# Two transformer blocks on one core: reciprocals, modulation parts, output slab quarters and first maxima in another order

## The chip, the cores and the metric

The kernel runs on 1 core of one Trainium2 chip. The metric is the device time of one execution in microseconds (us). The engines are TensorE (PE; its weight loads are PEld), VectorE (DVE), ScalarE (ACT), GpSimd (POOL) and SyncE (SP), which here only issues DMAs.

## What is computed

A first block with adaptive modulation, a token mixer of sparse attention (8 heads of 64, keys chosen by an indexer) beside a short convolution, and a SwiGLU; then a second block of two layers: gated linear attention, and differential attention (8 heads of two score maps each), each followed by a SwiGLU and a gated per-layer term. There are 256 tokens of width 1024, all in float32. The two parts that matter here, cut down:

```python
# first block, per 128-query block: the chosen keys are the causal top 64 of the indexer's scores
logits = einsum('bqhd,bqkd->bhqk', q_b, kg) * attn_scale
p = softmax(where(valid, logits, NEG_INF)); o = einsum('bhqk,bqkd->bqhd', p, vg)
mod = silu(c) @ w_ada + b_ada            # 6144 columns: shifts, scales and gates
mixed = concat([group_rms_norm(attn), group_rms_norm(gate_b * conv)]) @ w_out
# differential attention, per head: two softmaxes, their difference, values
o = (softmax(q1 @ k1.T) - lam * softmax(q2 @ k2.T)) @ v      # then rms_norm per head, then @ w_out
```

## The kernel before

The whole program is written out by hand for each engine. Every engine has one in-order stream, and semaphores join the streams; nothing is reordered by a compiler. All activations lie transposed, 128 channels x 256 tokens a tile, eight tiles a tensor.

**Weight slabs.** A large product takes its weights as slabs of 128 x 4096 values (2 MB). For a product at float32 precision a slab and its operand are split into a high and a low part (`whi`, `wlo`; `ohi`, `olo`), and TensorE runs three matmuls for each pair of tiles (`three`, L2219 to L2221). A slab is split in four quarters of 1024 columns. ScalarE writes the high quarter (`split`, called by `ahead`, L899), VectorE the low one (`low`, L1464); `lo_ready` counts the low quarters, and SyncE loads the next slab into a raw buffer when it is free. `ahead(ph, at, 0)` first waits until the slab that lies in the high buffer has been used by TensorE.

**Modulation parts.** The product `silu(c) @ w_ada` is done by VectorE. Its last eight slabs come in parts of 512 KB, four to a slab, and `modulate_part(n)` (L1561, L1563) adds part n: two operations of 512 columns, each chained to the next. `part_used` counts the parts done. TensorE sums a finished slab over its partitions (`modulation(i)`). On SyncE part 18 and 19 are loaded early; part 20 waits for `part_used` 19 (part 18 done), 21 for 20, 22 for 21, 23 for 22. SyncE's order around them is: parts 18, 19, 20, then `load_out(1)` (the second slab of the first block's output product, `out_w1`, which itself waits for `part_used` 18), then parts 21, 22, 23, then the first slab of `gate_up0`.

**Heads of the first block** (i = 0 to 7). TensorE: scores of head i+1; a projection of 16 matmul records (`in_hc` for i below 4, then `in_gb`); in head 5 the group sums of the first squares; the transposes of head i (`turned`, L2501), which need the scaled probabilities; the values of head i-1; now and then a modulation slab; in head 6 the group sums of `mix_sq` 2 (L2333), which need ScalarE's squares. ScalarE: scale head i's probabilities (L1075, waits for `inverted`), exponentials of head i+1 (L1063, wait for `max_ready`), `beside_head(i)`, the copy of the transposes (`prob_t`). `beside_head` has in heads 5 and 6 a high quarter of `out_w1`, and in head 6 the squares of tiles 4 and 5 ahead of it. VectorE: the loop that the diff changes, with `masked_maxima` (L1704, L1707), `invert_sums` (L1714), the convolution (L1650 to L1653) or the gated product (L1676), the low quarters and the parts. In heads 5 and 6 it has `low(PH["out0"], At(1), i - 5)`, which waits for ScalarE's high quarter.

**Differential heads** (i = 0 to 7, and three rounds to drain). TensorE: scores of head i+1 (L2820), values of head i-2 (L2835), six steps of the value projection (`value_steps`), transposes of head i-1 (L2846). Scores of head i+1 use the banks of head i-1 and wait for its exponentials. ScalarE: exponentials of head i (L1409), the copy of the transposes of head i-1 (L1425), in rounds 2, 5 and 7 `take_values` (L1385), then the high quarter of the output slab. VectorE: maxima of head i (L2166, L2169), the copy of head i-3's output (L2173), the probabilities of head i-1 (L2178 to L2185), then a low quarter. Before the heads stand `turn(6)` and `turn(7)`, the last two rotations of the keys (L2128, L2132), which take a product from GpSimd (L859).

Of the kernel before, what the change touches and what calls it, by code (L numbers as in the profile page):

```python
# [35 lines left out]
HD = 64  # L36
# [236 lines left out]
def build(nc, a, out):  # L273

    ctx = ExitStack()
    with ctx:
# [592 lines left out]
        def _(act):  # L869
# [32 lines left out]
            def ahead(ph, at, q):  # L902

                nxt = follow(ph, at)
                if nxt is None:
                    return
                if q == 0:

                    wait(act, tile_done, at.lin(ph.tile0, ph.tiles))
                split(*nxt, q)  # L910
# [490 lines left out]
            for i in range(NH + 1):  # L1401
                if i < NH:
                    me.next(max_ready)
                    for c in range(2):
                        for qt in range(2):
                            n = 4 * (i % 2) + 2 * c + qt
                            if i >= 2:
                                act.wait_ge(trans_done, NH + i - 1)
                            ins = act.activation(tl(d_p, 4 * (i % 2) + 2 * c + qt),  # L1409
                                                 G[2 * (i % 2) + c][:, qt * T:(qt + 1) * T], ACT.Exp,  # L1410
                                                 bias=neg_max[:, n:n + 1], scale=HD ** -0.5,
                                                 accum_out=sums[:, n:n + 1])
                        me.did(ins, exp_done)
                if i == 5:
                    squares((0,), d_o, d_nsq)
                if i == 7:
                    pair_root(0, X[1])
                    squares((1,), d_o, d_nsq)
                if i >= 1:
                    me.next(trans_done)  # L1420
                    if i == 1:
                        act.wait_ge(qk_ready, 8)
                    if i >= 3:
                        act.wait_ge(pv_done, NH + i - 2)
                    me.did(act.activation(tl(d_pt, (i - 1) % 2, w=512), X[0][:, :], ACT.Copy), pt_ready)  # L1425
                if i in (2, 5, 7):
                    take_values({2: 1, 5: 2, 7: 3}[i])
                if 1 <= i <= 4:
                    ahead(*OUT2, i - 1)
            wait(act, tile_done, PH["diff_v"].tile0 + 4)  # L1430
            high_parts_of(0, 1)
            pair_root(1, X[1])
# [22 lines left out]
        def _(dve):  # L1455
            me = Steps(dve, dve_step)

            def low(ph, at, q):

                slot, w = (ph.slot + at.parity) % 2, ph.cols // 4  # L1460
                hslot = (ph.j0 + at.parity) % 2
                src = out_w[hslot] if ph.name == "out0" else raw[slot]
                dve.wait_ge(hi_ready, at.lin(4 * ph.j0 + q + 1, 4))
                dve.tensor_tensor(wlo[hslot][:, q * w:(q + 1) * w], src[:, q * w:(q + 1) * w],  # L1464
                                  whi[hslot][:, q * w:(q + 1) * w].bitcast(F32), ALU.subtract).then_inc(lo_ready, 1)
# [245 lines left out]
            def invert_sums(i):  # L1711
                me.next(exp_done)
                s = i % 2
                me.did(dve.reciprocal(rsum[:, 2 * s:2 * s + 2], sums[:, 2 * s:2 * s + 2]), inverted)  # L1714

            PARTS_OF_HEAD = ((11, 12), (13, 14), (15, 16), (17, 18), (19, 20), (21,), (22,), (23,))
            me.again()
            masked_maxima(0)
            for q in range(2):
                low(PH["out0"], At(0), q)  # L1720
            modulate_part(10)
            for i in range(NH):
                invert_sums(i)
                if i + 1 < NH:
                    masked_maxima(i + 1)
                if i == 6:
                    mix_norm(0, 1)
                if i == 7:
                    mix_low(0, 1)
                if i in (1, 2):  # L1730
                    low(PH["out0"], At(0), i + 1)
                if i < 4:
                    short_conv(i)
                else:
                    gated_conv(i - 4)
                    if i in (5, 6):
                        low(PH["out0"], At(1), i - 5)
                for n in PARTS_OF_HEAD[i]:
                    modulate_part(n)
            dve.wait_ge(mod_done, 9)  # L1740
# [404 lines left out]
            VALUES, OUT2 = (PH["diff_v"], At(1)), (PH["out2"], At(0))  # L2145
            low(*VALUES, 0)
            low(*VALUES, 1)
            turn(6)
            turn(7)
            make_tile = group_make(d_o, d_nsq, lambda t: lam[:, 5:6])  # L2150

# [7 lines left out]
                    me.did(low_part(t, tl(om, t), xhi, xlo), olo_ready)  # L2159

            for i in range(NH + 3):
                if i < NH:
                    me.next(score_done)
                    s = 4 * (i % 2)
                    for c in range(2):
                        me.did(dve.tensor_reduce(neg_max[:, s + 2 * c:s + 2 * c + 2],  # L2166
                                                 v3(G[2 * (i % 2) + c][:, :], 2), AX, ALU.max, negate=True))
                    me.again()
                    me.did(dve.tensor_scalar(neg_max[:, s:s + 4], neg_max[:, s:s + 4], HD ** -0.5, None, ALU.mult),  # L2169
                           max_ready)  # L2170
                if i >= 3:
                    me.next(pv_done)
                    me.did(dve.tensor_copy(tl(d_o, i - 3), X[2][:, 0:T]), mixed_ready)  # L2173
                if 1 <= i <= NH:

                    me.next(exp_done, 2)
                    s = 4 * ((i - 1) % 2)
                    me.link(dve.reciprocal(rsum[:, s:s + 4], sums[:, s:s + 4]))  # L2178
                    me.did(dve.tensor_scalar(rsum[:, s + 2:s + 4], rsum[:, s + 2:s + 4], lam[:, 4:5], None, ALU.mult))
                    for qt in range(2):  # L2180
                        me.did(dve.tensor_scalar(tl(d_p, s + qt), tl(d_p, s + qt), rsum[:, s + qt:s + qt + 1],
                                                 None, ALU.mult))
                    me.again()
                    for qt in range(2):
                        ins = dve.scalar_tensor_tensor(tl(d_p, s + qt), tl(d_p, s + 2 + qt),  # L2185
                                                       rsum[:, s + 2 + qt:s + 3 + qt], tl(d_p, s + qt),
                                                       ALU.mult, ALU.add)
                    me.did(ins, prob_ready)
                if i == NH:
                    wait(dve, tile_done, PH["diff_v"].tile0 + 4)  # L2190
                    make_pair(0)
                if i == NH + 1:
                    low_pair(0)
                if i in (0, 1):
                    low(*VALUES, 2 + i)
                if 2 <= i <= 5:
                    low(*OUT2, i - 2)
            for g in range(1, 4):
                make_pair(g)
                if g > 1:  # L2200
# [699 lines left out]
```

## Time and profile before

| what | value |
|---|---|
| median of 3 runs | 1079.1 us (1078.55 to 1080.32) |
| the profiled execution | 1077.96 us, its span 1076.2 us |
| TensorE busy | 1042.4 us, 97% of the span |
| VectorE, ScalarE, GpSimd busy | 731.7, 552.9, 202.2 us |
| mean granted TensorE clock | 0.995 |
| chain that ended last | PE 56%, DVE 5%, ACT 3%, issue 1% |

The page gives shares over the whole span. For an order change the useful views are the engines' waits in a stretch, and the timeline of one engine in that stretch. In a timeline the bracket behind an instruction is the time that its engine stood idle before it, and what released it.

### The profile page before, as it was taken

The page shows a single profiled execution, that of the slowest core. Times are in us where ns is not written, and L with a number is a line of the kernel's source. Part 1 is how long each engine was busy: PE and PEld are TensorE (multiplying, and loading weights), DVE is VectorE, ACT ScalarE, POOL GpSimd, SP SyncE. Part 2 cuts the span into 40 slices and gives each one's busy share as a digit, 9 for nine tenths or more (in the row PEclk, how much of TensorE's full clock was granted, in tenths as well). Part 3 has the DMA queues.
Part 4 walks back from the last instruction along what each step waited for, and adds up shares of the span by engine and source line. Part 5 has one row for each costly group of instructions (what it writes and reads, how often), then busy time and mean ns, then how long its engine had stood idle before and what let it go on. Part 6 is the DMA issues. An engine that isn't in the chain of part 4 may idle for free.

```text
span 1076.2 us, 20430 instructions
## 1 busy us (share of the span) xinstructions
PE 1042.4 (97%) x7993; PEld 981.9 (91%) x7993; DVE 731.7 (68%) x1155; ACT 552.9 (51%) x946; POOL 202.2 (19%) x223
## 2 busy tenths in 40 slices
PE   5999999999999999999999999999989999999998
PEld 5577788999999998989999999998877999999998
DVE  5798777767654788868556555686787765564565
ACT  2223457545363585527454444566467764544453
POOL 0000012233311001022333321021210223322010
PEclk9999999999999999999999999999999999999999
DMA  9993453577556454504564546654322265644661
GB/s 350 399 389 121 169 184 98 195 254 262 174 168 190 137 192 173 183 2 153 186 209 156 174 131 203 247 185 157 131 105 79 93 222 178 212 132 140 185 208 40
DMA packets 183587, 192.78 MB, mean 179 GB/s; under 512 B 5913, under 2 KB 143426, under 8 KB 183522
## 3 DMA queue, kind: packets, MB, share of 16 engines
q1 hardware_dynamic: 182512, 191.15, 52.5%
q8 instruction: 43, 0.70, 0.3%
q0 software_dynamic: 144, 0.52, 0.2%
q10 hardware_dynamic: 866, 0.21, 0.1%
q14 instruction: 22, 0.18, 0.0%
HBM read 190.83 MB, written 1.05 MB: 178 GB/s over the span
## 4 chain that ended last, share of the span: by engine, by line
PE 56%; DVE 5%; ACT 3%; issue 1%; POOL 0%; DVEq 0%; POOLq 0%; ACTq 0%
PE gemm L2219 17%; PE gemm L2221 17%; PE gemm L2220 16%; DVE wlo L1464 1%; PE aux L2717 1%; PE aux L2835 1%; PE aux L2767 1%; ACT whi L899 1%; DVE prod L1943 1%; PE gemm L2820 1%; PE aux L2773 0%; PE aux L2219 0%; DVE state L2075 0%; PE aux L2221 0%; PE aux L2220 0%
## 5 line engine op out<-in xcount | busy, mean ns | idle before, releaser
L2219 PE MATMUL gemm<-ohi,whi 128*128 128x256 f32 x1376 | 389.5, 283 | 3.8 <-issue 1.1
L1464 DVE TENSOR_TENSOR wlo<-raw,whi 128x1024 fp32r<-128x1024 f32 (+1 forms) x308 | 352.2, 1187 | 58.8 <-ACT whi L899 58.1
L2220 PE MATMUL gemm<-olo,whi 128*128 128x256 f32 x1376 | 385.8, 280 | 0.0
L2221 PE MATMUL gemm<-ohi,wlo 128*128 128x256 f32 x1376 | 383.6, 279 | 0.0
L899 ACT ACTIVATE whi<-raw 128x1024 fp32r<-128x1024 f32 (+1 forms) x308 | 276.4, 963 | 60.4 <-PE gemm L2221 44.2
L2219 PEld LDWEIGHTS gemm<-ohi,whi 128*128 128x128 f32 x1376 | 259.1, 188 | 6.7 <-DVE wlo L1464 2.8
L2220 PEld LDWEIGHTS gemm<-olo,whi 128*128 128x128 f32 x1376 | 259.5, 189 | 0.6 <-issue 0.5
L2221 PEld LDWEIGHTS gemm<-ohi,wlo 128*128 128x128 f32 x1376 | 259.4, 189 | 0.0
L2221 PE MATMUL gemm<-acthi,wlo 128*128 128x256 f32 x528 | 147.8, 280 | 0.0
L2219 PE MATMUL gemm<-acthi,whi 128*128 128x256 f32 x528 | 147.5, 279 | 0.0
L2220 PE MATMUL gemm<-actlo,whi 128*128 128x256 f32 x528 | 147.3, 279 | 0.0
L755 POOL TENSOR_TENSOR prod<-sg,ut 128x256 f32<-128x256 f32 x66 | 51.2, 777 | 265.1 <-DVE ut L1888 161.0
L2220 PEld LDWEIGHTS gemm<-actlo,whi 128*128 128x128 f32 x528 | 99.3, 188 | 0.0
L2221 PEld LDWEIGHTS gemm<-acthi,wlo 128*128 128x128 f32 x528 | 99.1, 188 | 0.0
L2219 PEld LDWEIGHTS gemm<-acthi,whi 128*128 128x128 f32 x528 | 98.8, 187 | 0.0
L1194 ACT ACTIVATE sg<-gt 128x256 f32<-128x256 f32 x66 | 27.6, 419 | 132.9 <-DVE gt L1888 91.4
L759 POOL TENSOR_TENSOR actlo<-prod,acthi 128x256 f32 (+1 forms) x63 | 70.3, 1116 | 0.0
L2220 PE MATMUL gemm<-xlo,whi 128*128 128x256 f32 x224 | 62.6, 279 | 0.0
L1888 DVE TENSOR_TENSOR ut<-gemm,rstd 128x256 f32<-128x256 f32 x44 | 18.4, 418 | 52.1 <-PE gemm L2221 52.1
L782 POOL TENSOR_TENSOR sq_sum<-sq_sum,dsq 128x256 f32<-128x256 f32 x28 | 24.0, 856 | 111.3 <-ACT dsq L924 99.2
L2220 PEld LDWEIGHTS gemm<-xlo,whi 128*128 128x128 f32 x224 | 42.2, 188 | 1.9 <-issue 1.9
L2448 PE MATMUL gemm<-om,raw 128*128 128x256 f32 x192 | 43.6, 383 | 0.0
(383 smaller groups left out, 1549.0 us busy)
## 6 DMA issues: line engine op xcount, KB each, us to landing
raw<-in_ffn_w_in SPq DMA_DIRECT2D x44, 1024.0 KB, 6.2
raw<-in_ffn_w_out SPq DMA_DIRECT2D x32, 704.0 KB, 5.2
part<-in_w_ada SPq DMA_DIRECT2D x32, 512.0 KB, 10.7
raw<-in_gla_w_in SPq DMA_DIRECT2D x6, 2048.0 KB, 7.8
raw<-in_diff_w_in SPq DMA_DIRECT2D x6, 2048.0 KB, 7.9
raw<-in_w_gate SPq DMA_DIRECT2D x11, 1024.0 KB, 6.3
raw<-in_w_up SPq DMA_DIRECT2D x11, 1024.0 KB, 8.5
raw<-in_w_down SPq DMA_DIRECT2D x16, 704.0 KB, 5.2
```

Source lines behind the costliest of these rows:

```text
L755: pool.tensor_tensor(tl(prod, j), tl(sg, j), tl(ut, j), ALU.mult).then_inc(prod_done, 1)
L759: pool.tensor_tensor(tl(actlo, t - 1), tl(prod, 1 - j), tl(acthi, t - 1).bitcast(F32), ALU.subtract).then_inc(actlo_ready, 1)
L782: pool.tensor_tensor(sq_sum[:, :], sq_sum[:, :], src, ALU.add).then_inc(squares_summed if last else sq_added, 1)
L899: act.activation(whi[hslot][:, q * w:(q + 1) * w], src[:, q * w:(q + 1) * w], ACT.Copy).then_inc(hi_ready, 1)
L1194: act.activation(tl(sg, j), tl(gt, j), ACT.Silu).then_inc(silu_done, 1)
L1464: dve.tensor_tensor(wlo[hslot][:, q * w:(q + 1) * w], src[:, q * w:(q + 1) * w], whi[hslot][:, q * w:(q + 1) * w].bitcast(F32), ALU.subtra ...
L1888: ins = dve.tensor_tensor(dst, bank[:, 0:T], rstd[:, 0:T], ALU.mult)
L1943: me.link(dve.tensor_tensor(tl(prod, t % 2), tl(sg, t % 2), pp(k, t), ALU.mult))
L2219: pe.matmul(dst, st_hi, mv_hi, start=start, stop=False)
L2220: pe.matmul(dst, st_hi, mv_lo, start=False, stop=False)
L2221: return pe.matmul(dst, st_lo, mv_hi, start=False, stop=stop_)
L2448: ins = pe.matmul(G[t][:, 0:T], w[:, k, t * P:(t + 1) * P], tl(om, k), start=k == 0, stop=k == KT - 1)
```

## The change

In the first block's heads the reciprocal of the next head's sums (`invert_sums(i + 1)`) moves ahead of this head's modulation parts, and that of head 0 between the first two low quarters. Parts 12, 14, 16, 18 and 20 each move one head later. The third and fourth low quarters of the first output slab move from heads 1 and 2 to heads 2 and 4. In the differential heads the four high quarters of the output slab move from rounds 1 to 4 to rounds 2 to 5 on ScalarE, and the low ones from rounds 2 to 5 to rounds 3 to 6 on VectorE. The maxima of head 0 move ahead of `turn(7)`. No instruction is added or removed.

```diff
-                if 1 <= i <= 4:
-                    ahead(*OUT2, i - 1)
+                if 2 <= i <= 5:
+                    ahead(*OUT2, i - 2)
...
-            PARTS_OF_HEAD = ((11, 12), (13, 14), (15, 16), (17, 18), (19, 20), (21,), (22,), (23,))
+            PARTS_OF_HEAD = ((11,), (12, 13), (14, 15), (16, 17), (18, 19), (20, 21), (22,), (23,))
             me.again()
             masked_maxima(0)
-            for q in range(2):
-                low(PH["out0"], At(0), q)
+            low(PH["out0"], At(0), 0)
+            invert_sums(0)
+            low(PH["out0"], At(0), 1)
             modulate_part(10)
             for i in range(NH):
-                invert_sums(i)
                 if i + 1 < NH:
                     masked_maxima(i + 1)
                 if i == 6:
                     mix_norm(0, 1)
                 if i == 7:
                     mix_low(0, 1)
-                if i in (1, 2):
-                    low(PH["out0"], At(0), i + 1)
                 if i < 4:
                     short_conv(i)
                 else:
                     gated_conv(i - 4)
-                    if i in (5, 6):
-                        low(PH["out0"], At(1), i - 5)
+                if i + 1 < NH:
+                    invert_sums(i + 1)
+                if i in (2, 4):
+                    low(PH["out0"], At(0), 1 + i // 2)
+                if i in (5, 6):
+                    low(PH["out0"], At(1), i - 5)
                 for n in PARTS_OF_HEAD[i]:
                     modulate_part(n)
...
+            def maxima(i):
+
+                me.next(score_done)
...
             turn(6)
+            maxima(0)
             turn(7)
...
-                if i < NH:
...
+                if 1 <= i < NH:
+                    maxima(i)
...
-                if 2 <= i <= 5:
-                    low(*OUT2, i - 2)
+                if 3 <= i <= 6:
+                    low(*OUT2, i - 3)
```

## Rows read from the trace of the kernel before

**Rows 1.** The page, part 1: busy time, share of the span, instructions.

```profile
PE 1042.4 (97%) x7993; PEld 981.9 (91%) x7993; DVE 731.7 (68%) x1155; ACT 552.9 (51%) x946; POOL 202.2 (19%) x223
```

**Rows 2.** TensorE's waits, 84 to 150 us: us in total, times, longest.

```profile
PE aux L2501 <- ACT logit L1075: 2.8, 3, 1.3
```

**Rows 3.** Timeline of TensorE, first heads: start, us, instruction, idle before.

```profile
112.13 0.52 PE L2501 MATMUL aux<-const,logit 128*128 128x128 f32 x3 [1.29 <-ACT logit L1075]
...
133.46 1.10 PE L2333 MATMUL gemm<-mix_sq,const 128*128 128x512 f32 x2 [0.32 <-ACT mix_sq L1069]
```

**Rows 4.** Timeline of TensorE, differential heads.

```profile
788.18 2.22 PE L2820 MATMUL gemm<-d_k,d_q 64*128 64x256 f32 x16
...
794.07 1.13 PE L2820 MATMUL gemm<-d_k,d_q 64*128 64x256 f32 x8 [1.32 <-ACT d_p L1409]
...
797.36 0.60 PE L2846 MATMUL aux<-const,d_p 128*128 128x128 f32 x4
...
804.57 1.78 PE L2820 MATMUL gemm<-d_k,d_q 64*128 64x256 f32 x8 [1.91 <-ACT d_p L1409]
```

**Rows 5.** Timeline of VectorE, first heads, heads 3 to 6.

```profile
114.08 3.12 DVE L1563 SCALAR_TENSOR_TENSOR acc_b<-part,c_act,acc_b 128x512 f32<-128x512 f32 x4
117.23 0.17 DVE L1714 RECIPROCAL rsum<-sums 128x2 f32<-128x2 f32 x1
...
118.97 0.42 DVE L1676 TENSOR_TENSOR mixed<-gemm,conv 128x256 f32<-128x256 f32 x1 [0.45 <-PE gemm L2448]
...
121.22 0.49 DVE L1561 TENSOR_SCALAR acc_a<-part,c_act 128x512 f32<-128x512 f32 x1 [0.39 <-DMA part<-in_w_ada]
...
122.53 0.17 DVE L1714 RECIPROCAL rsum<-sums 128x2 f32<-128x2 f32 x1
...
127.77 1.22 DVE L1464 TENSOR_TENSOR wlo<-out_w,whi 128x1024 fp32r<-128x1024 f32 x1 [2.76 <-ACT whi L899]
128.92 1.53 DVE L1563 SCALAR_TENSOR_TENSOR acc_a<-part,c_act,acc_a 128x512 f32<-128x512 f32 x2
130.48 0.17 DVE L1714 RECIPROCAL rsum<-sums 128x2 f32<-128x2 f32 x1
130.57 0.56 DVE L1704 SCALAR_TENSOR_TENSOR logit<-aux,allow 128x384 f32<-128x384 f32 x1
...
131.69 0.87 DVE L1691 SCALAR_TENSOR_TENSOR mixed<-mixed,cols_a,mix_sq 128x256 f32<-128x256 f32 x2
```

**Rows 6.** Timeline of SyncE: the loads of part 20 and of the second output slab.

```profile
117.22 0.37 SPq L640 DMA_DIRECT2D part<-in_w_ada  x1
117.63 0.47 SPq L657 DMA_DIRECT2D out_w<-in_w_out  x1
```

**Rows 7.** Tile out_w, 100 to 140 us: issue to landing of the second slab.

```profile
DMA to landing us min/median/max: 8.7/8.7/8.7
```

**Rows 8.** Timeline of ScalarE, first heads: high quarter of `out_w1`, squares of tiles 4 and 5.

```profile
126.70 1.04 ACT L899 ACTIVATE whi<-out_w 128x1024 fp32r<-128x1024 f32 x1
...
132.70 0.61 ACT L1069 ACTIVATE mix_sq<-mixed 128x512 f32<-128x512 f32 x1
```

**Rows 9.** Window table: stretch, its length, each engine busy, PEclk, DMA.

```profile
804.50:808.10 3.60, 3.53 (x13) 2.56 (x13) 3.49 (x10) 3.60 (x11) 0.00 (x0) 0.56 0.03 10
```

**Rows 10.** Timeline of VectorE, start of the differential heads.

```profile
789.87 0.69 DVE L2132 TENSOR_TENSOR d_k<-d_t,d_t 128x512 f32<-128x512 f32 x1 [0.65 <-POOL d_t L859]
790.47 1.28 DVE L2166 TENSOR_REDUCE neg_max<-gemm 128x2 f32<-128x512 f32 x2
...
795.39 0.88 DVE L2185 SCALAR_TENSOR_TENSOR d_p<-d_p,rsum 128x256 f32<-128x256 f32 x2
```

**Rows 11.** Timeline of ScalarE, differential heads 0 to 2.

```profile
792.00 0.47 ACT L1409 ACTIVATE d_p<-gemm,neg_max 128x256 f32<-128x256 f32 x1 [2.87 <-DVE neg_max L2169]
...
801.54 1.06 ACT L899 ACTIVATE whi<-raw 128x1024 fp32r<-128x1024 f32 x1 [2.95 <-PE aux L2221]
802.51 0.46 ACT L1409 ACTIVATE d_p<-gemm,neg_max 128x256 f32<-128x256 f32 x1
```

More of the change, by code:

```diff
@@ L2147, in _ @@
             low(*VALUES, 1)
+            def maxima(i):
+                me.next(score_done)
+                s = 4 * (i % 2)
+                for c in range(2):
+                    me.did(dve.tensor_reduce(neg_max[:, s + 2 * c:s + 2 * c + 2],
+                                             v3(G[2 * (i % 2) + c][:, :], 2), AX, ALU.max, negate=True))
+                me.again()
+                me.did(dve.tensor_scalar(neg_max[:, s:s + 4], neg_max[:, s:s + 4], HD ** -0.5, None, ALU.mult),
+                       max_ready)
             turn(6)
+            maxima(0)
             turn(7)
@@ L2161, in _ @@
             for i in range(NH + 3):
-                if i < NH:
[L2163 to L2170, printed above, removed]
+                if 1 <= i < NH:
+                    maxima(i)
                 if i >= 3:
```

## The prediction

> **What bounds the kernel now.** I read the page's busy times first: TensorE is busy for 97% of the span [rows 1]. The kernel is one long stream of TensorE work in program order, so an edit counts only where TensorE waits, or where it makes TensorE wait. Then I read TensorE's waits in the two stretches that the diff touches. In the eight heads of the first block (84 to 140 us) it waits for the scaled probabilities before the transposes of heads 0, 2 and 3, 2.8 us in all [rows 2], 1.29 us of it in head 3 [rows 3]. In the differential heads (788 to 831 us) two waits matter: 1.32 us before the scores of head 2 and 1.91 us before those of head 4, both for the exponentials on ScalarE [rows 4]. Last I read VectorE's, ScalarE's and SyncE's own order in both stretches, because what is moved there sets when buffers and semaphores come. The numbers below are of one execution; a step "after" is its start before, moved by the steps ahead of it.
>
> **Part 1: the reciprocals.** ScalarE scales head i's probabilities only after `invert_sums(i)`, which stands behind all `modulate_part` calls of the head before: in head 3 the four sums of parts 17 and 18 begin at 114.08 and the reciprocal starts only at 117.23 [rows 5]. The change puts it ahead of them. No instruction is added. The 2.8 us of waits end, and nothing comes late in heads 0 to 3: VectorE has the reciprocal out some 3 us before TensorE's projection ends. If that were all, this part would give 2.8 us (up to 3.6, since each wait also costs the restart behind it).
>
> **Part 2: parts and lows of the first block are pushed back.** Parts 12, 14, 16, 18 and 20 each move one head later, the low quarters 2 and 3 of the first output slab from heads 1 and 2 to heads 2 and 4. The lows have cover until 139 us. The parts do not, and the reason is on SyncE's queue. It is in order: part 20's load waits until part 18 is consumed (117.22, the moment at which VectorE ends it), and behind it at 117.63 stands the load of the second output slab, `out_w1` [rows 6]. Moving part 18 from head 3 to head 4 therefore moves a 2 MB load that the diff never names.
> How late is part 18? At 117.23 VectorE had finished it. After the change it must first also do head 4's maxima (130.57 to 131.69 for such a set, 1.1 us), the gated product (0.4) and two reciprocals (0.09 each from start to next start) [rows 5]: 118.9. It also meets two new waits. TensorE is now the slower of the two in head 2 (about 0.7 us for the projection's last matmul), and head 4's exponentials end 2.2 us after its maxima begin while only 1.4 us of VectorE's work stands between (0.8 us). Together: part 18 ends near 120.4, and 119 to 121.5 are the bounds. `out_w1` goes out at 120.8 instead of 117.63.
> It took 8.7 us to land [rows 7], that is until 126.3, and ScalarE began its high part at 126.70 [rows 8]: it was in time by 0.4 us, with nothing to spare. After the change it lands at 129.5 and ScalarE starts at 129.6. The Trainium skill (DMA: Bandwidth & Descriptors, "Anatomy of one DMA — SWDGE (gpsimd) path") fits a DMA by about 2.0 us and 436 GB/s, which for 2 MB would be an estimated 6.8 us; by it the slab would not be late until 2 us later and the first block would lose 2 us less. The row has 8.7 us, with part 20 ahead on the same queue, and the row decides.
> Behind that high part wait two engines. ScalarE must finish it before it copies head 5's transposes and scales head 6. VectorE stands in head 5 at the low of this quarter; before, it waited 2.76 us there, then did part 21 and began head 7's maxima at 130.57 [rows 5]. Now it goes: high part 129.6, low 130.7, then part 20 as well as 21. Part 20 took 1.31 us from its start at 121.22 to the next reciprocal at 122.53 [rows 5], so head 7's maxima begin 2.9 + 1.3 - 0.1 = 4.1 us later, at 134.7. Head 7's exponentials follow them, the squares of the gated tiles follow those (132.70 before [rows 8]), and TensorE's group sums need the squares: they already waited 0.32 us for them at 133.46 [rows 3]. After: 137.6. All that the reciprocals gave has gone into this wait, and the first block is 4.1 us behind; 0.2 us come back at head 7's transposes. **First block: +3.9 us**, bounds +2.5 and +5.
> TensorE then idles about 3 us before head 6's transposes and 4.4 us before the group sums. What such a gap costs beyond itself has one clear row: after the wait of 1.91 us at 804.57 the granted clock is 0.56 over 804.50 to 808.10 [rows 9], so some 3.2 us went at 1.2 GHz and lost 1.6 us against 2.4 GHz. I take the same price here, with bounds of 0.8 (the low stretch partly inside the gap) and 2.6: **+1.7 us**.
>
> **Part 3: first maxima between the last turns.** Head 0's scores are done at about 789.3, half way through the sixteen matmuls that begin at 788.18 [rows 4], but the maxima begin only at 790.47, behind turn 7, whose last step stood there for GpSimd [rows 10]. Moved ahead of it they begin at 789.35, and head 0's exponentials (792.00 before [rows 11]) 1.1 us earlier; of the 1.32 us wait 0.2 stays. Turn 7 ends later by the maxima's 1.4 us less the wait for GpSimd, and everything behind it on VectorE shifts by +0.26. So head 0's probabilities, ready at 795.39 + 0.88 = 796.27 [rows 10], come at 796.5, and TensorE's transposes move from 797.36 [rows 4] to 796.6. **-0.8 us**; with the bounds 0 and -1.3.
>
> **Part 4: output slab quarters one differential head later.** The first quarter's high part waits until the first value slab is used up (tile 1 of the values, 801.5). It stands in head 1 in ScalarE's queue, ahead of head 2's exponentials: 2.95 us idle, high part 801.54, exponentials 802.51 [rows 11], and TensorE waits 1.91 us for them at 804.57 [rows 4]. One head later head 2's exponentials run as soon as their maxima allow: these begin near 797.6, exponentials follow 1.5 us behind the start of the maxima (790.47 to 792.00 [rows 10, 11]) and take 1.9 us, so they end at 801.0, while TensorE asks for them at 801.8, and the wait goes. Next late would be head 3's exponentials: ScalarE first takes the copy (to 802.5), the values (0.7) and the quarter (1.0 [rows 11]) and ends them at 806.0. TensorE asks at 806.5, one round of 4.7 us after 801.8. The last quarter now falls in head 5 on ScalarE, behind `take_values(2)`, and in head 6 on VectorE, each in slack. The next load into that slab's buffer, `gate_up2`, goes out about 1 us later and is needed 30 us after that. **-1.9 us**, and with the wait its half-clock stretch [rows 9], **-1.6**. Bounds of the two together: -1.5 (a new wait of head 3 takes part, clock falls elsewhere) and -3.7.
>
> **Sum.** First block +3.9 and +1.7, second -0.8, -1.9 and -1.6: **+1.3 us** against the profiled execution's 1077.96 us (span 1076.2), that is 1079.3. The median of the three runs is 1079.1, 1.1 above this profile. The clock term at 804.57 may not stand in every run at its full price, as the runs scatter over 1.8 us; I count 0.2 less gain for it. Forecast for the median: 1079.1 + 1.5 = **1080.6 us**.
>
> **Rivals.**
> - *Forecast (0.50)*: two opposite shifts that nearly cancel. Its own range is 1079 to 1082.
> - *Slower, the clock is paid twice (0.25)*. The two gaps in the first block are parted by barely 1.2 us of matmuls, so the array may resume at 1.2 GHz and be still in a second low stretch through the last projection and the start of the output product. Price 1.6 us more and no relief in the second block's other clock losses: 1079.1 + 3.9 + 3.3 - 4.1 = 1082.2. It decides as soon as the low clock after the group sums lasts longer than about 4 us. For it: a single 1.91 us gap was enough at 804.57; against it: gaps of 1.29 and 1.32 us left the clock at full. The Trainium skill (TensorE: Matmul & The Clock Gate, "HAM oscillation — how this bites in real kernels") tells of a kernel in which every burst between waits started cold; by that rule this rival's time is the one.
> - *Faster, the slab is not late (0.15)*. If VectorE reaches part 18 earlier or the slab lands earlier than in the row, the group sums wait less. With a shift of 1.5 us instead of 4.1 and no clock loss: 1079.1 + 1.5 - 4.1 = 1076.5; with none and the reciprocals' gain kept, 1079.1 - 2.8 - 4.3 = 1072. Against it: 126.3 to 126.70 left only 0.4 us.
> - *The second block gives little (0.10)*: head 3's exponentials make a wait as long as that removed, only part 3's 0.8 us stays: 1079.1 + 5.6 - 0.8 = 1083.9.
>
> **Range and chances.** A measurement of this kernel can tell about 0.2%, 2.2 us, from no change: 1076.9 to 1081.3. Range 1076.5 to 1083.4: it leaves out the far end of the faster rival and most of the last one. Slower: all of the last, 0.8 of the clock rival and a small part of the forecast, 0.37. Faster: 0.13. Same: 0.50.
>
> **What would show it.** SyncE's issue of `out_w1` near 120.8 and ScalarE's first high part of the second slab near 129.6, now with a DMA as releaser; no waits of TensorE for scaled probabilities in heads 0 to 3, but one of some 4 us at the group sums and one of 3 us before head 6's transposes; a granted clock near 0.5 after 137.6. In the second block the transposes of head 2 some 4.3 us earlier relative to the block's start, no wait at head 4's scores and full clock. The forecast is wrong if the slab's issue moved by less than 2 us, if the group sums are not what waits, or if head 3's exponentials are late in the second block.

## The result

The changed kernel takes **1080.83 us** (median of 20 runs, 1079.16 to 1082.85) against 1078.74 us (1077.57 to 1080.87) of the kernel before in the same job: ratio 1.002, 95% interval 1.0014 to 1.0026. It is slower by 2.1 us. That is small, but the interval does not reach 1. The median given for `e4_warm` below leaves out one slow execution of 1728.75 us at a granted clock of 0.558. The span of the profiled execution is 1080.1 us.

To place the difference I use two **blocks**, each read within one trace. The first block runs from head 0's maxima to head 7's transposes, the second from the scores of differential head 0 to the transposes of head 2. Lines behind the edits move by up to 8 in the changed kernel (TensorE's L2501 is now L2509, L2333 is L2341, L2820 is L2828).

| | first block | second block | median |
|---|---|---|---|
| before | 52.55 us | 22.17 us | 1078.74 us |
| changed | 58.90 us | 18.36 us | 1080.83 us |
| difference | +6.35 | -3.81 | +2.1 |

The blocks add up to +2.5 us. The spans differ by 3.9 us, because the changed kernel's profiled execution also reached head 0's maxima 1.57 us later (87.17 against 85.60 us). In the profiles below that moment lies between 85.6 and 87.5 us whatever the edit, so it is the scatter of the start. Take 1.57 off a time of the changed kernel's first block before you compare it with a row of before.

TensorE's waits from 84 to 150 us, changed kernel (us in total, times, longest). The 2.8 us of [rows 2] were spread over heads 0, 2 and 3. Now there are none in these heads, but one long wait in head 6's transposes and a longer one before the group sums, which had waited 0.32 us [rows 3].

```profile
PE gemm L2341 <- ACT mix_sq L1069: 4.4, 1, 4.4
PE aux L2509 <- ACT logit L1075: 3.2, 1, 3.2
```

TensorE's timeline there. The group sums took 1.10 us in [rows 3] and take 2.05 now:

```profile
133.12 0.52 PE L2509 MATMUL aux<-const,logit 128*128 128x128 f32 x3 [3.24 <-ACT logit L1075]
...
138.85 2.05 PE L2341 MATMUL gemm<-mix_sq,const 128*128 128x512 f32 x2 [4.41 <-ACT mix_sq L1069]
140.69 5.55 PE L2456 MATMUL gemm<-om,raw 128*128 128x256 f32 x16
146.07 0.49 PE L2509 MATMUL aux<-const,logit 128*128 128x128 f32 x3
```

The window table of the same stretch (length, TensorE busy, granted clock, DMA share, GB/s). The clock falls inside the gap, is at 0.50 while TensorE works without a pause, and is back behind 144.5:

```profile
134.00:139.00 5.00, 0.59 (x4) 0.53 0.53 140
139.00:144.50 5.50, 5.50 (x11) 0.50 1.01 345
144.50:149.00 4.50, 4.38 (x26) 0.99 0.65 239
```

What the two waits follow from, engine by engine: VectorE waits for exponentials and adds parts 18 and 19 (the first two rows of its timeline), SyncE issues part 20 and the second output slab, the slab lands, ScalarE makes its high quarter, VectorE the low one, two parts, and then head 7's maxima.

```profile
121.83 0.37 SPq L640 DMA_DIRECT2D part<-in_w_ada  x1
122.25 0.47 SPq L657 DMA_DIRECT2D out_w<-in_w_out  x1
```
```profile
DMA to landing us min/median/max: 8.6/8.6/8.6
```
```profile
130.85 1.06 ACT L899 ACTIVATE whi<-out_w 128x1024 fp32r<-128x1024 f32 x1 [3.98 <-DMA out_w<-in_w_out]
...
138.09 0.61 ACT L1069 ACTIVATE mix_sq<-mixed 128x512 f32<-128x512 f32 x1
```
```profile
119.07 0.17 DVE L1714 RECIPROCAL rsum<-sums 128x2 f32<-128x2 f32 x1 [0.72 <-ACT logit L1063]
...
120.28 3.10 DVE L1563 SCALAR_TENSOR_TENSOR acc_b<-part,c_act,acc_b 128x512 f32<-128x512 f32 x4
...
131.94 1.22 DVE L1464 TENSOR_TENSOR wlo<-out_w,whi 128x1024 fp32r<-128x1024 f32 x1 [6.11 <-ACT whi L899]
133.09 0.48 DVE L1561 TENSOR_SCALAR acc_a<-part,c_act 128x512 f32<-128x512 f32 x1
133.60 2.33 DVE L1563 SCALAR_TENSOR_TENSOR acc_a<-part,c_act,acc_a 128x512 f32<-128x512 f32 x3
135.96 0.56 DVE L1704 SCALAR_TENSOR_TENSOR logit<-aux,allow 128x384 f32<-128x384 f32 x1
```

Read the brackets from bottom to top. VectorE stood 6.11 us for ScalarE, which stood 3.98 us for the transfer. In the kernel before ScalarE's high quarter had no DMA in its bracket [rows 8].

The second block, TensorE in the changed kernel. The scores of head 2 (801.66) and of head 4 (810.20) follow without a wait, where [rows 4] had 1.32 and 1.91 us, and the window 803 to 811 has a granted clock of 1.00 where [rows 9] had 0.56:

```profile
796.01 2.23 PE L2828 MATMUL gemm<-d_k,d_q 64*128 64x256 f32 x16
...
801.66 1.13 PE L2828 MATMUL gemm<-d_k,d_q 64*128 64x256 f32 x8
...
804.96 0.60 PE L2854 MATMUL aux<-const,d_p 128*128 128x128 f32 x4
...
810.20 1.13 PE L2828 MATMUL gemm<-d_k,d_q 64*128 64x256 f32 x8
```
```profile
803.00:811.00 8.00, 8.00 (x64) 1.00 0.56 182
```

One wait is new, and my working did not have it (TensorE's waits, 790 to 820 us):

```profile
PE aux L2227 <- DVE d_t L2130: 1.1, 1, 1.1
```

The operation that it waits for is turn 7's read of a PSUM bank (`aux`) on VectorE. In the kernel before, this read starts 0.34 us behind the start of head 0's scores (788.18 [rows 4]); in the changed kernel it starts 2.59 us behind it, after head 0's maxima. The rows are VectorE's before, then VectorE's and TensorE's in the changed kernel:

```profile
788.52 0.69 DVE L2128 TENSOR_TENSOR d_t<-aux,const 128x512 f32<-128x512 f32 x1
```
```profile
798.60 0.69 DVE L2130 TENSOR_TENSOR d_t<-aux,const 128x512 f32<-128x512 f32 x1
```
```profile
799.35 0.39 PE L2227 MATMUL aux<-whi,dhi 128*128 128x256 f32 x1 [1.11 <-DVE d_t L2130]
```

### The profile page after: what moved, and what is told of

Same layout as the page of the kernel before. It is cut to its first block, busy times and chain, and to the rows that moved or that the text cites. A ratio compares the mean times of both kernels' runs of the same rounds, so it can differ in the third digit from the quotient of the medians.

```text
span 1080.1 us, 20427 instructions
## 1 busy us (share of the span) xinstructions
PE 1044.4 (97%) x7993; PEld 983.5 (91%) x7993; DVE 731.9 (68%) x1155; ACT 552.6 (51%) x946; POOL 202.2 (19%) x223
## 4 chain that ended last, share of the span: by engine, by line
PE 57%; DVE 5%; ACT 2%; issue 1%; DVEq 0%; ACTq 0%
PE gemm L2227 17%; PE gemm L2229 17%; PE gemm L2228 17%; DVE wlo L1464 1%; PE aux L2725 1%; PE aux L2843 1%; PE aux L2775 1%; PE aux L2781 1%; PE gemm L2828 1%; PE aux L2227 1%; DVE prod L1945 1%; ACT whi L899 1%; PE aux L2229 1%; PE aux L2228 1%; DVE state L2077 0%
## 5 line engine op out<-in xcount | busy, mean ns | idle before, releaser
L2456 PEld LDWEIGHTS gemm<-om,raw 128*128 128x128 f32 x192 | 37.4, 198 | 8.9 <-issue 3.8
```

The lines of the kernel that those rows point to most:

```text
L2456: ins = pe.matmul(G[t][:, 0:T], w[:, k, t * P:(t + 1) * P], tl(om, k), start=k == 0, stop=k == KT - 1)
```

## Experiments

Each kernel was timed in five rounds beside the kernel before; "faster" and "slower" are differences of the two medians of one job. The medians of before were 1078.41 us for the first four kernels, 1079.09 for the next four, 1079.07 for the three behind them and 1078.52 for the last.

### Which half does what: e1_first, e2_second

`e1_first` has the edits of the first block alone, `e2_second` those of the differential heads alone.

```diff
 # e2_second: the changed kernel with the first block's loop of before
-            PARTS_OF_HEAD = ((11,), (12, 13), (14, 15), (16, 17), (18, 19), (20, 21), (22,), (23,))
+            PARTS_OF_HEAD = ((11, 12), (13, 14), (15, 16), (17, 18), (19, 20), (21,), (22,), (23,))
...
-                if i + 1 < NH:
-                    invert_sums(i + 1)
```

> The first block's edits alone (reciprocals, parts, low quarters); the differential heads as before. Theory (late slab load, then a half-clock stretch): 6 us slower than before, about 1084.7, with TensorE's waits of some 3.2 us before head 6's transposes and 4.4 us at the group sums. Rival (the profile of the changed kernel was an unlucky run, the first block costs about nothing): within 1 us of before.

> The differential heads' edits alone; the first block as before. Theory: 3.8 us faster than before, about 1074.9, with no wait of TensorE before the scores of heads 2 and 4 but one of 1.1 us at the value steps behind head 1's scores. Rival (the gain seen in the one profile was the clock that happened to fall in before): 2 us faster or less.

Measured: `e1_first` 1083.14 us, 4.7 slower (ratio 1.0043, 1.003 to 1.0056), first block 57.65 us. `e2_second` 1074.57 us, 3.8 faster (0.996, 0.9948 to 0.9973), first block 52.55 as before, second 18.39. So the small net figure is a loss and a gain, each larger than itself. They lie in different blocks, but the runs don't show that they add exactly: the two medians give +0.9 us together, the changed kernel measured +2.1, and the intervals allow both. The loss was 1.3 us less than I expected. In this run's profile the group sums are as late as in the changed kernel (51.72 against 51.68 us behind head 0's maxima), but from them to head 7's transposes it takes 5.93 us instead of 7.22. Its second block, which has no edit, is also 1.6 us shorter than before (20.58 us), since the clock did not fall there; the last section comes back to this.

### What makes the first block long: e3_slab_ahead

```diff
-                      ("in_gb", 0): [*parts(18, 19, 20), lambda: load_out(1), *parts(21, 22, 23)],
+                      ("in_gb", 0): [*parts(18, 19), lambda: load_out(1), *parts(20, 21, 22, 23)],
```

> The changed kernel with one edit more: on SyncE's queue the second output slab's load goes ahead of part 20's, so that it waits for part 17 only. Theory (the load stuck behind part 20 is the whole loss): issue near 115.5 us plus the run's offset, no wait of TensorE before head 6's transposes, at most 0.5 us at the group sums, no low clock there; first block 3 us faster than before instead of 6 slower, in all about 1072. Rival (VectorE's order is the loss: part 20 now stands in head 5 ahead of head 7's maxima, and it comes later behind the slab): the group sums still wait over 1 us, in all 1076 or more.

Measured: 1076.82 us, 1.6 faster than before (0.998, 0.997 to 0.9989), thus some 3.7 us better than the changed kernel, but far from 1072. First block 55.36 us. The slab now lands in time, and head 6's transposes no longer wait. The group sums still do:

```profile
PE gemm L2341 <- ACT mix_sq L1069: 3.8, 1, 3.8
```

They start 49.28 us after head 0's maxima (47.86 before, 51.68 in the changed kernel). So the late slab made 2.4 us of the 3.8 by which they were late. The stretch from them to head 7's transposes is shorter too, 6.08 us against 7.22, but `e1_first` has 5.93 with the gap of the changed kernel, so this can be scatter of the clock. For the rest read VectorE in this kernel:

```profile
128.83 1.22 DVE L1464 TENSOR_TENSOR wlo<-out_w,whi 128x1024 fp32r<-128x1024 f32 x1 [2.01 <-ACT whi L899]
129.97 0.48 DVE L1561 TENSOR_SCALAR acc_a<-part,c_act 128x512 f32<-128x512 f32 x1
130.48 2.32 DVE L1563 SCALAR_TENSOR_TENSOR acc_a<-part,c_act,acc_a 128x512 f32<-128x512 f32 x3
132.84 0.56 DVE L1704 SCALAR_TENSOR_TENSOR logit<-aux,allow 128x384 f32<-128x384 f32 x1
```

Parts 20 and 21, 2.8 us of work, stand ahead of head 7's maxima in head 5; before it was part 21 alone, 1.5 us [rows 5]. And ScalarE takes its high quarter only behind head 6's exponentials and a root, so VectorE waits 2.01 us, although the slab landed 2.1 us before ScalarE took it up (issue 117.78, 7.9 us to land, high quarter 127.75). My range for "no lateness" (1072) forgot that; the rival came true in part.

### What the clock costs: e4_warm

Matmuls on constants fill most of the two gaps (0.7 and 0.8 us of wait are left); nothing else moves.

```diff
+                if i == 6:
+                    keep_warm(G[3], 3)
                 turned(i)
                 if i:
                     values(i - 1)
+                if i == 6:
+                    keep_warm(G[3], 4)
```

> The changed kernel with dummy matmuls of 512 columns into a free bank while TensorE waits: three before head 6's transposes and four behind head 6's values. They change nothing but the activity (the waits are about 3.2 and 4.4 us, a dummy of this size about 0.9 us). Theory (the half-clock stretch behind the two gaps costs about 2.5 us beyond the gaps themselves): the last projection at full clock, 2 to 2.5 us faster than the changed kernel, about 1078.5. Rival (the clock's cost is hidden behind other engines): the same 1080.8.

Measured: 1078.77 us (ratio to before 1.0, 0.9991 to 1.0009). That is 0.4 us slower than before where the changed kernel is 2.1 slower, so some 2 us better than it (1.7 by the medians, 2.2 by the two ratios). The group sums come at the same distance from head 0's maxima (51.76 against 51.68 us), so the gap is untouched. What changed is the time from them to head 7's transposes: 4.38 us instead of 7.22 (4.69 before):

```profile
138.74 1.10 PE L2341 MATMUL gemm<-mix_sq,const 128*128 128x512 f32 x2 [0.79 <-ACT mix_sq L1069]
139.67 3.62 PE L2456 MATMUL gemm<-om,raw 128*128 128x256 f32 x16
```

The low clock behind the gap is thus a cost by itself: 2.8 us in the profile against this run (2.5 against before, where the same stretch took 0.3 us more), and some 2 us in the medians.

### The two edits of the second block: e6_maxima, e7_quarters

Both have the first block of before. `e6_maxima` keeps the quarters of before, `e7_quarters` keeps the first maxima of before.

```diff
 # e6_maxima, against the kernel before
             turn(6)
+            maxima(0)
             turn(7)
...
-                if i < NH:
+                if 1 <= i < NH:
 # e7_quarters, against the kernel before (and so for low, 3 <= i <= 6)
-                if 1 <= i <= 4:
-                    ahead(*OUT2, i - 1)
+                if 2 <= i <= 5:
+                    ahead(*OUT2, i - 2)
```

> Part 3 alone: head 0's maxima between turn(6) and turn(7), with the first block and the slab quarters of the kernel before. Theory (the wait moves): the maxima start 1.3 us sooner, but turn(7)'s read of its PSUM bank then comes 1.3 us later, and the value steps of the next tile want that bank, so that TensorE waits some 1.1 us there; of part 3 only 0.2 us is left, the rest of the differential block is as before, and the kernel is 0.0 to 0.3 us faster than before (1.000). Rival (the maxima carry the gain of 3.8): with the first rows out sooner no gap of 1.9 us comes before the scores of head 4, TensorE's clock stays up, and the block from the scores of head 0 to the transposes of head 2 shrinks by over 2 us.

> Part 4 alone: the output slab's quarters one differential head later on ScalarE and VectorE, the first block and the order of the first maxima as in the kernel before. Theory (quarters and clock carry the gain): the wait of 1.9 us ahead of head 4's scores goes, and with it the stretch at the lower granted clock (1.6 us); the block from the scores of head 0 to the transposes of head 2 takes 18.4 to 18.9 us (22.2 before), the kernel is 3.2 to 3.8 us faster than before (0.9965 to 0.997). Rival (both parts are needed): with the maxima late ScalarE stays behind, a wait of over 1 us is left ahead of head 4's scores and the clock falls as before; then the kernel is at most 1.5 us faster.

Measured: `e6_maxima` 1079.52 us, no difference (1.0007, 0.9993 to 1.0021), second block 21.95 us: 0.2 less than before. Its waits in the differential heads:

```profile
PE gemm L2826 <- ACT d_p L1409: 1.9, 1, 1.9
PE aux L2225 <- DVE d_t L2128: 1.1, 1, 1.1
...
```

The wait of 1.32 us is gone, one of 1.1 us stands in its place, the 1.91 us remain. `e7_quarters` 1075.44 us, 3.65 faster (0.9974, 0.9957 to 0.9992), second block 18.60 us: 3.6 less. So the quarters carry nearly the whole gain of the second block.

### The reciprocals alone: e8_recip

```diff
 # against the kernel before
-            for q in range(2):
-                low(PH["out0"], At(0), q)
+            low(PH["out0"], At(0), 0)
+            invert_sums(0)
+            low(PH["out0"], At(0), 1)
...
-                invert_sums(i)
...
+                if i + 1 < NH:
+                    invert_sums(i + 1)
+                if i >= 4:
...
                 for n in PARTS_OF_HEAD[i]:
                     modulate_part(n)
```

> Kernel before with the first block's reciprocals alone moved ahead of the modulation sums (the reciprocal of each head behind the conv of the head before, head 0's between the two slab parts); the modulation parts keep their heads, the slab's low parts theirs, the differential block is as before. Theory (the lateness of part 18 makes the loss): part 18 stays in head 3, the out slab is issued as early as in the kernel before or up to 0.7 us sooner, there is no wait of 3 us ahead of head 6's transposes, and the waits of 1.29 and 0.32 us of the kernel before shrink: 0 to 2 us faster than before (0.998 to 1.000). Rival (the reciprocals' place itself costs): the block from head 0's maxima to head 7's transposes is over 2 us longer than the 52.6 us of before, and the kernel is 2 us or more slower.

Measured: 1078.31 us, not to be told from before (ratio 1.0, 0.999 to 1.0009). First block 52.64 us against 52.55. The waits of heads 0, 2 and 3 are gone, and one of 2.1 us is new at the group sums:

```profile
PE gemm L2336 <- ACT mix_sq L1069: 2.1, 1, 2.1
```

The reciprocal's new place is harmless, and worth nothing: what TensorE no longer waits in heads 0 to 3 it waits at the group sums, since VectorE is not sooner there: the group sums start 48.25 us behind head 0's maxima, against 47.86 before. The slab was issued 32.8 us after head 0's maxima, against 32.0 before and 35.1 in the changed kernel. The loss of the first block thus comes from what this run leaves in place, the parts and the two low quarters of the first slab. No run moves the low quarters alone. The rows of the result and `e3_slab_ahead` lead to the parts: as many low quarters stand ahead of part 18 in the changed kernel as before.

### Repairs: e9_split_turn, e12_parts, e13_squares, e14_second_split, e15_all

`e9_split_turn` lets turn 7 read its PSUM bank ahead of the maxima and do its sum behind them.

```diff
             turn(6)
+            me.next(qk_rot)
+            me.again(qk_ready)
+            me.did(dve.tensor_tensor(v3(d_t2[:, :], 2), v3(X[3][:, :], 2), bc(C("sin_d", T), 2), ALU.mult),
+                   qk_rot_read)
             maxima(0)
-            turn(7)
+            me.next(qk_cos)
+            me.again(qk_rot_read)
+            me.did(dve.tensor_tensor(pair(7), d_t1[:, :], d_t2[:, :], ALU.add), qk_ready)
```

> The changed kernel with turn(7) cut in two on VectorE: its read of the PSUM bank first, then head 0's maxima, then its sum. Theory: the bank comes free as soon as in the kernel before, so the new wait of 1.1 us of the value steps goes, and the maxima start 0.6 us later than in the changed kernel but 0.7 us sooner than before; the differential block is 0.3 to 0.9 us shorter than in the changed kernel, the kernel 1.4 to 1.8 us slower than before instead of 2.1 (1.0013 to 1.0017). Rival (the bank is not what ends that wait): the wait stays 1 us and the time is the changed kernel's or 0.5 us more.

Measured: 1080.27 us, 1.2 slower than before (1.0013, 1.0003 to 1.0023), where the changed kernel is 2.1 slower. Second block 17.50 us against 18.36. VectorE reads the bank at 794.62 and begins the maxima 0.84 us later, and TensorE's wait for the bank is gone; what is left is 0.2 us before head 2's scores. The maxima are no later for it: they start 1.18 us behind the start of head 0's scores (794.28), in the changed kernel 1.19, because VectorE had stood idle there. The medians alone don't tell this run from the changed kernel (1.0013 and 1.002, with intervals that overlap); the wait and the block in the trace do. The rows are VectorE's:

```profile
794.62 0.69 DVE L2165 TENSOR_TENSOR d_t<-aux,const 128x512 f32<-128x512 f32 x1
795.46 1.29 DVE L2156 TENSOR_REDUCE neg_max<-gemm 128x2 f32<-128x512 f32 x2
...
796.87 0.69 DVE L2170 TENSOR_TENSOR d_k<-d_t,d_t 128x512 f32<-128x512 f32 x1
```

`e12_parts` and `e13_squares` stand on `e3_slab_ahead` and take away, in two ways, what was left there.

```diff
 # e12_parts
-            PARTS_OF_HEAD = ((11,), (12, 13), (14, 15), (16, 17), (18, 19), (20, 21), (22,), (23,))
+            PARTS_OF_HEAD = ((11,), (12, 13), (14, 15), (16, 17), (18, 19), (), (20, 21), (22, 23))
 # e13_squares, ScalarE
-                if i == 6:
-                    group_squares(2, gated_ready, 2)
                 if i in (5, 6):
                     split(PH["out0"], At(1), i - 5)
+                if i == 5:
+                    group_squares(2, gated_ready, 2)
```

> The kernel with the slab ahead of part 20 (e3_slab_ahead), and parts 20 and 21 moved from head 5, where they stand ahead of head 7's maxima on VectorE, to head 6 behind them; parts 22 and 23 both in head 7. Theory (what the slab's issue had not given back is VectorE's order): head 7's maxima come 2.8 us sooner (three products and one scaling between the slab's low part and the maxima in e3_slab_ahead), the wait of 3.75 us before the group sums shrinks to about 1 us, the clock stays up, and the block from head 0's maxima to head 7's transposes takes 51 to 52.6 us instead of 55.4: 3 to 4.5 us faster than e3_slab_ahead, 5 to 6.5 us faster than before (0.994 to 0.9955). Rival (another wait is next, as the slab was): the maxima come sooner but the squares or a transfer hold the group sums, the block shrinks by under 1 us and the time is that of e3_slab_ahead (0.998).

> The kernel with the slab ahead of part 20 (e3_slab_ahead), and on ScalarE the squares of the gated pair moved from behind head 7's exponentials to ahead of them, behind the slab quarter. Theory: the chain slab quarter, VectorE's parts, maxima, exponentials, squares, group sums is cut at its last link: the group sums wait for nothing, TensorE has its projection of 3.6 us before it needs head 7's probabilities and waits 1.5 to 2.5 us there; the block from head 0's maxima to head 7's transposes takes 51 to 52.5 us instead of 55.4: 3 to 4.5 us faster than e3_slab_ahead (0.994 to 0.9955 against before). Rival (the same lateness is only paid one step later): the transposes wait as long as the group sums did, the clock falls all the same, and the kernel is within 1 us of e3_slab_ahead.

Measured: `e12_parts` 1076.22 us, 2.9 faster than before (0.9976, 0.9963 to 0.999). The first block is 50.79 us, better than expected, with 0.9 us of wait before the group sums; VectorE's order was what was left. But of the 4.6 us that this block is shorter than in `e3_slab_ahead`, the medians show 1.3, with intervals that overlap, and the trace shows who takes the rest back. VectorE now waits for the loads of parts 22 and 23, the low parts of the operand come late, and TensorE waits for them at the output product:

```profile
139.06 1.54 DVE L1563 SCALAR_TENSOR_TENSOR acc_a<-part,c_act,acc_a 128x512 f32<-128x512 f32 x2 [1.02 <-DMA part<-in_w_ada]
141.66 1.54 DVE L1563 SCALAR_TENSOR_TENSOR acc_a<-part,c_act,acc_a 128x512 f32<-128x512 f32 x2 [1.06 <-DMA part<-in_w_ada]
```
```profile
144.88 0.39 PE L2227 MATMUL gemm<-ohi,whi 128*128 128x256 f32 x1 [1.85 <-DVE olo L1513]
```

Behind this wait the granted clock is low (window table, 0.64):

```profile
144.80:149.00 4.20, 4.12 (x23) 0.64 1.06 393
```

From head 0's maxima to the scores of differential head 0 it takes 703.07 us, against 702.58 before and 705.19 in `e3_slab_ahead`: against before, all of the 1.8 us of the block is gone again. My range of 5 to 6.5 us for this kernel missed that.

`e13_squares` 1073.64 us, 5.4 faster than before (0.9943, 0.9925 to 0.9961). First block 49.96 us. The group sums wait for nothing, and the one wait left is 1.6 us at head 7's transposes:

```profile
131.12 1.13 PE L2341 MATMUL gemm<-mix_sq,const 128*128 128x512 f32 x2
132.09 3.62 PE L2456 MATMUL gemm<-om,raw 128*128 128x256 f32 x16
137.32 0.52 PE L2509 MATMUL aux<-const,logit 128*128 128x128 f32 x3 [1.62 <-ACT logit L1075]
```

Here nothing is taken back: from head 0's maxima to the scores of differential head 0 it takes 699.98 us, 2.6 less than before, as the block is.

> Both edits of the differential heads, with turn(7) cut in two as in e9_split_turn, and the first block of the kernel before. Theory: the two gains add, since nothing is shared: 3.8 us of e2_second and 0.9 us of the split (block 17.5 us from the scores of head 0 to the transposes of head 2): 4.7 us faster than before (0.9952 to 0.996). Rival: the split gains only behind the late first block, and the kernel is that of e2_second (0.9963).

`e14_second_split` 1073.82 us, 5.2 faster (0.9952, 0.9938 to 0.9967): second block 17.51 us, first 52.55. In the block the split adds 0.9 us to the gain of `e2_second` (18.39); the two medians can't be told apart (0.9952 and 0.996, the intervals overlap).

> The changed kernel with the three repairs: the slab ahead of part 20 on SyncE's queue, the squares of the gated pair ahead of head 7's exponentials (both as in e13_squares), and turn(7) cut in two (as in e9_split_turn). Theory (the repairs lie in different blocks and add): the first block takes 50.0 us as in e13_squares (52.6 before), the differential block 17.5 as in e9_split_turn (22.2 before), so 7.2 us less than before on paper; e13_squares measured 6.2 of its own 6.4, so 6.5 to 7.2 us faster than before (0.9933 to 0.994). Rival: behind a shorter first block the out projection waits for its operands, and a part of the gain is given back; then it is within 0.3 us of e13_squares (0.9943 or more).

`e15_all`, the changed kernel with the three repairs, 1071.02 us, **7.5 us faster than before** (0.9935, 0.9921 to 0.9948). First block 49.96 us, second 17.49. It is the best kernel of the study.

## Why the prediction was right, and where it was not

The forecast was 1080.6 us, measured 1080.83. The way it came about was the one forecast, two opposite shifts; two of its terms were off, the clock by 0.8 us and the first maxima by 0.6, and both made the kernel slower than the sum.

**Part 1 (2.8 us of waits end).** Right, and `e8_recip` shows it alone: no wait for scaled probabilities in heads 0 to 3. Also right that this is not a gain by itself; but I gave the late slab as the only reason. With the slab's issue only 0.8 us later than before, `e8_recip` still gave everything back at the group sums.

**Part 2, the slab.** Take off 1.57 us for the start. Issue of `out_w1` 122.25 (predicted 120.8 + 1.57 = 122.4), landing 8.6 us (8.7 [rows 7]), high part at 130.85 (131.2), head 7's maxima at 135.96 (136.3), group sums 3.82 us later than before (4.1). The two waits that I took from TensorE's and ScalarE's pace, 0.7 and 0.8 us, came as well: 0.54 us before head 2's convolution on VectorE, and 0.72 us in the bracket of the reciprocal at 119.07, both ahead of part 18. The Trainium skill's fit of a DMA ("Anatomy of one DMA — SWDGE (gpsimd) path" in DMA: Bandwidth & Descriptors) would have had an estimated 6.8 us for the slab. It is a fit for loads that GpSimd issues, and SyncE issues these; the landing in these traces was 8.6 and 8.7 us with a part ahead of it on the queue, and 7.9 us in `e3_slab_ahead` with none just ahead. The measured rows decided rightly.

**Part 2, the clock.** The term that was mis-sized: +1.7 us predicted, 2.5 measured in the block (from the group sums to head 7's transposes 7.22 us against 4.69), 2.8 against `e4_warm`, and 1.7 to 2.2 in the medians. It scatters: the same stretch behind a gap of the same kind took 2.3 us more than before in `e9_split_turn` (6.94) and 1.2 in `e1_first` (5.93), so the 1.7 was less wrong than this one profile says. I priced it at one low stretch of 3.6 us by [rows 9]; the work at 0.50 lasted from 138.85 to about 144.3 us. The rival "paid twice" came in part. By the sign that I had set for it (low clock after the group sums for longer than about 4 us) it holds, with 5.5 us. Its price of +3.3 us does not: it is one low stretch through the last projection and no second one, and the clock is full again before the output product starts at 147.29. The measured 2.5 lies between the two prices, so my sign would not have told them apart.

**First block in sum.** +5.6 us predicted, +6.35 measured.

**Part 3 (the first maxima).** -0.8 us predicted; measured -0.22 in `e6_maxima` alone, and -0.24 as the changed kernel's second block against that of `e7_quarters`. That is inside its bounds, but the step is wrong. I wrote that turn 7 "ends later" and costs only what stands behind it on VectorE. Turn 7 also reads a PSUM bank, and TensorE's next value steps write into this bank. The read came 2.25 us later behind head 0's scores (1.4 us of maxima and some 0.9 us in which VectorE waited for the scores), not 1.3 as I wrote for `e6_maxima`. Before, it had ended over 1 us before TensorE needed the bank, so TensorE waited 1.1 us for it. `e9_split_turn` confirms this: with the read ahead of the maxima the wait goes and the block is 0.86 us shorter than in the changed kernel.

**Part 4 (the quarters).** -1.9 and -1.6 us predicted, together -3.5; `e7_quarters` gave -3.6 in the block and -3.65 in the medians. Head 3's exponentials, which I had named as the next to be late, were not.

**The sum.** +1.3 us from the blocks (+1.5 for the median) predicted, +2.5 in the blocks and +2.1 in the medians measured. That the forecast time is so close is partly luck: the difference was 0.6 us too small, and the start of the sum was 0.4 us too high, since the three runs from which it starts had a median of 1079.1 and the twenty of the comparison 1078.74.

## What to carry to other kernels

When work moves later on one engine, look for each semaphore that it counts, and for everything that stands behind a wait for this semaphore on a DMA queue: here one part moved by one head delayed a 2 MB load that the edit never names, and this was most of the loss (3.7 us of the medians came back in `e3_slab_ahead`). An instruction that reads a PSUM bank gives it back when it has run, so moving something ahead of it moves TensorE's next write to this bank. And a wait that ends in one place is a gain only if the engine that was late is sooner there as well; `e8_recip` and `e12_parts` removed waits of nearly 3 us, and the next wait took them back.

## What the hardware did unexpectedly

The length of a gap did not decide whether TensorE's granted clock fell. The same wait of 1.91 us before the scores of head 4 was followed by a clock of 0.56 in the kernel before [rows 9], of 0.65 in `e6_maxima` and 0.63 in `e8_recip`, and by 1.00 in `e1_first`. The code of this stretch is the same in the kernel before and in `e1_first`, and the granted clock was 1.00 ahead of the wait in both. The wait of 1.6 us at head 7's transposes was followed by 0.67 in `e13_squares` and by 1.00 in `e15_all`, which has the same first block. The window rows are, in this order, of `e1_first`, `e13_squares` and `e15_all`:

```profile
810.90:814.50 3.60, 3.56 (x25) 1.00 0.04 14
```
```profile
137.30:141.60 4.30, 4.28 (x21) 0.67 1.08 383
```
```profile
136.70:141.00 4.30, 4.14 (x29) 1.00 1.07 381
```

So a gap of 1.6 to 1.9 us is a risk and not a fixed price: nothing, or 1.6 us (second block 22.17 us before, 20.58 in `e1_first`), or 1.2 us in `e13_squares` (its next value step, head 7's, starts 55.75 us behind head 0's maxima, 54.60 in `e15_all`). Even that need not reach the end: at the scores of differential head 0 these two are only 0.2 us apart (699.98 and 699.80). The Trainium skill ("HAM oscillation — how this bites in real kernels" in TensorE: Matmul & The Clock Gate) tells of bursts between waits that each start cold, behind waits longer than these. Here the burst behind the gap of 4.41 us did start at 0.50, but the burst of 1.2 us behind the gap of 3.24 us had 1.00 (from 133 to 134 us), and behind gaps of 1.6 to 1.9 us these traces show both. Why `e1_first` and the kernel before differ is not settled by these runs.
